# A one-core hybrid encoder layer: the front put in another order (rows turned as they land, indexer first, scoring and heads beside projections, bias table made early)

## The chip, the core and the metric

The kernel runs on one core of one Trainium2 chip. It is written by hand for the core's engines: TensorE multiplies matrices (PE in the profile; PEld is its weight load), VectorE (DVE), ScalarE (ACT) and GpSimd (POOL) do the rest, SyncE (SP) issues most DMAs. The metric is device time in microseconds (us) from start to end of one launch, and the median of several runs is quoted.

## What is computed

One layer of a streaming encoder is applied to 256 prompt rows and 32 sample rows, all in float32 and handled as one block of T = 288 columns. The reference, cut to what matters here:

```python
u = _rmsnorm(x, lw['g_attn'])
zA, zq, zk, zv, ziq, zik, ziw, zmq, zg = _split(u @ lw['w_in'], IN_SIZES)
o_a, new_shift, new_wkv = _rwkv7_time_mix(zA, shift0, wkv0, lw)
...
dots = jnp.einsum('bthd,bsd->bths', iqs, ik_all)
score = jnp.einsum('bths,bth->bts', jax.nn.relu(dots), iws).astype(jnp.float32)
_, idx = lax.top_k(score, topk)
...
logits = jnp.einsum('btngd,btsnd->btngs', qg, ks).astype(jnp.float32) * (HD_B ** -0.5)
bias = rel_bias[_t5_bucket(idx - ps[None, :, None])].astype(jnp.float32)
...
mk, mv = _split(_rmsnorm(mem_prompt, g_mem[l]) @ w_mem_kv[l], (D_M, D_M))
o_m = _memory_attention(zmq.reshape(B, T, H_M, HD_M), mem_k, mem_v)
...
mixed = (gates[:, :, 0] * (o_a @ lw['p_a']) + gates[:, :, 1] * (o_b @ lw['p_b'])
         + gates[:, :, 2] * (o_m @ lw['p_m']))
h = x + mixed @ lw['w_o']
h = h + _hier_moe(_rmsnorm(h, lw['g_ffn']), lw)
```

The change concerns the part up to `o_m`, called the front here: the norm, most of the projection by `w_in`, the projection of the memory rows, the indexer (16 heads score the keys, the best quarter is kept), the 8 attention heads and the 4 heads into the memory.

## The kernel before

**Units of the projections.** A strip is 256 columns of a weight matrix (2 MB). SP loads strips into a ring of four slots, two DMAs of 1 MB each, and loads strip n when the multiplications with strip n - 4 are done. A strip makes two units of 16 matmuls; a unit puts 128 columns of the weights against all 288 rows (for the memory projection 128 memory rows against 256 columns) and is copied out of one of two PSUM banks by ACT. There are 72 units: 16 of the memory projection, 56 of `w_in`. Each matmul is two records in the trace. A quarter of a unit is four matmuls.

**Order before.** (1) The five blocks of rows land whole; ACT squares them, DVE scales them, PE turns them in 80 transposes (line 687), ACT copies them out (lines 1251 and 1253). (2) 16 units of the memory projection (line 703), then 32 transposes of memory keys (line 715). (3) 32 units of `w_in` (line 730). (4) The four memory heads for three blocks of rows (12 turns), with a quarter of one of the last 24 units put between their steps (line 752, `a_mms(1)`, three per turn). (5) The indexer and the heads: for each block of rows 16 scoring matmuls (line 814), whose results ACT clips (1344) and DVE adds up (1589), then top-k in rounds of `max` and `match_replace` on DVE, then 8 heads with two quarters each (lines 821, 829, 845). (6) The norms of the RWKV keys (lines 859 and 867). Then the loop over pairs of RWKV heads begins at line 910, and after it the rest (`p_a`, `w_o` at line 1055, the experts). Between (1) and (6) the engines PE, ACT and DVE wait for each other at the end of each part (`phase_end`, `phase_wait`). The units of the last 24 that carry RWKV columns ("raw" units) are blended by DVE with the row before (`mix`).

**The bias table.** Heads add a bias that depends on the distance of key and query. PE makes 8 rows of 640 numbers from a one-hot table (lines 802 and 803), DVE copies them to `brow`, and POOL writes each row 128 times to DRAM (`dram_bias`) and reads it back with a row pitch one shorter, so that every partition gets its own shift:

```python
pool.wait_ge(s("brow_done"), 1)
pload(dram_bias, brow[0:H_B, :].unsqueeze(1).to_broadcast([H_B, P, BW]), "brow_out")
pool.wait_ge(s("brow_out"), 16)
for h in range(H_B):
    src = bass.AP(tensor=dram_bias.tensor, offset=h * P * BW + 128, ap=[[BW - 1, P], [1, E_W]])
    pload(E[:, h, :], src, "E_in")
```

In part (5) DVE waits for `E_in` (line 1607) before the first head.

## Time and profile before

| | us |
|---|---|
| median of 3 runs (2344.91 to 2354.4) | 2348.91 |
| the profiled execution, its own time | 2346.51 |
| span of the profiled execution | 2344.9 |
| PE busy in it | 2144.5 (91%) |
| DVE, ACT, POOL busy | 536.4, 274.6, 62.9 |
| first record of the RWKV loop (line 910) | 800.37 |

The time outside the span is 1.6 us. A busy engine is one that has an instruction under way; PE's ends are modelled, so 91% is not 91% of its best. The trace also gives the clock that PE was granted: 1.00 is 2.4 GHz and 0.50 is 1.2 GHz.

### The profile page before, as it was taken

The page shows a single profiled execution, that of the slowest core. Times are in us where ns is not written, and L with a number is a line of the kernel's source. Part 1 is how long each engine was busy: PE and PEld are TensorE (multiplying, and loading weights), DVE is VectorE, ACT ScalarE, POOL GpSimd, SP SyncE. Part 2 cuts the span into 40 slices and gives each one's busy share as a digit, 9 for nine tenths or more (in the row PEclk, how much of TensorE's full clock was granted, in tenths as well). Part 3 has the DMA queues.
Part 4 walks back from the last instruction along what each step waited for, and adds up shares of the span by engine and source line. Part 5 has one row for each costly group of instructions (what it writes and reads, how often), then busy time and mean ns, then how long its engine had stood idle before and what let it go on. Part 6 is the DMA issues. An engine that isn't in the chain of part 4 may idle for free.

```text
span 2344.9 us, 30255 instructions
## 1 busy us (share of the span) xinstructions
PE 2144.5 (91%) x12647; PEld 1439.5 (61%) x12647; DVE 536.4 (23%) x1414; ACT 274.6 (12%) x645; POOL 62.9 (3%) x116
## 2 busy tenths in 40 slices
PE   5999999983899899999999999999999699999996
PEld 3887777762675677776767777677777333333332
DVE  1000000222455323232232322322100322122112
ACT  4010000210222201011010101100000100000002
POOL 0000000001000100000000000000000000000000
PEclk9999999995898799999999999999999799999998
DMA  7554434325222113323131322316643399999996
GB/s 237 179 179 144 128 124 123 108 86 104 95 73 65 51 38 113 108 78 113 38 113 60 111 89 76 110 37 241 209 132 137 142 428 427 427 427 427 427 428 273
DMA packets 189048, 404.86 MB, mean 173 GB/s; under 512 B 11328, under 2 KB 165648, under 8 KB 174928
## 3 DMA queue, kind: packets, MB, share of 16 engines
q1 hardware_dynamic: 181136, 380.95, 44.4%
q0 software_dynamic: 6688, 21.20, 3.2%
q8 instruction: 116, 1.90, 0.3%
q10 hardware_dynamic: 1088, 0.66, 0.1%
q14 instruction: 20, 0.16, 0.0%
HBM read 392.10 MB, written 10.67 MB: 172 GB/s over the span
## 4 chain that ended last, share of the span: by engine, by line
PE 81%; DMA 9%; DVE 3%; another core or an unknown queue 2%; issue 2%; ACT 1%; DVEq 1%; ACTq 0%; POOL 0%; SPq 0%
PE bank L891 17%; PE bank L730 11%; PE bank L752 7%; PE bank L1124 6%; PE bank L893 6%; PE bank L1055 5%; PE bank L703 5%; PE bank L1157 3%; PE bank L1174 3%; PE bank L1022 3%; DMA ring<-in_w 3%; DMA Z<-in_w 3%; DMA SC<-in_w 2%; PE bank L947 1%
## 5 line engine op out<-in xcount | busy, mean ns | idle before, releaser
L891 PE MATMUL bank<-uT,ring 128*128 128x288 f32 x1536 | 423.6, 427 | 0.0
L891 PEld LDWEIGHTS bank<-uT,ring 128*128 128x128 f32 x1536 | 292.5, 197 | 86.5 <-issue 5.0
L730 PE MATMUL bank<-uT,ring 128*128 128x288 f32 (+2 forms) x1024 | 248.9, 406 | 0.7 <-ACTq L340 0.7
L730 PEld LDWEIGHTS bank<-uT,ring 128*128 128x128 f32 (+2 forms) x1024 | 190.5, 186 | 58.8 <-ACTq L340 0.9
L752 PE MATMUL bank<-uT,ring 128*128 128x288 f32 x768 | 212.6, 424 | 0.0
L752 PEld LDWEIGHTS bank<-uT,ring 128*128 128x128 f32 x768 | 146.7, 198 | 43.6 <-issue 6.6
L1124 PE MATMUL bank<-ring,Z 128*64 128x512 f32 x480 | 138.5, 611 | 6.9 <-issue 6.9
L893 PE MATMUL bank<-Z,ring 128*128 128x288 f32 x512 | 138.9, 417 | 1.9 <-issue 1.9
L1055 PE MATMUL bank<-SC,ring 128*128 128x288 f32 x512 | 128.4, 409 | 1.1 <-DVEq L340 1.1
L1124 PE MATMUL bank<-Z 128*64 128x512 f32 x336 | 119.2, 614 | 5.0 <-issue 5.0
L1055 PEld LDWEIGHTS bank<-SC,ring 128*128 128x128 f32 x512 | 96.0, 190 | 29.6 <-DVEq L340 1.6
L703 PE MATMUL bank<-ring,Z 128*128 128x256 f32 x512 | 111.0, 379 | 1.9 <-ACT Z L1253 1.3
L893 PEld LDWEIGHTS bank<-Z,ring 128*128 128x128 f32 x512 | 92.7, 190 | 27.0 <-issue 2.8
L1509 DVE TENSOR_TENSOR SC<-SC 128x287 f32<-128x287 f32 (+1 forms) x27 | 12.3, 457 | 423.0 <-ACT SC L1287 373.7
L703 PEld LDWEIGHTS bank<-ring,Z 128*128 128x128 f32 x512 | 97.1, 190 | 15.6 <-issue 1.5
L1386 ACT ACTIVATE Z<-bank 128x288 f32<-128x288 f32 (+1 forms) x48 | 19.7, 410 | 603.1 <-PE bank L891 603.0
L1124 PEld LDWEIGHTS bank<-ring,Z 128*64 128x64 f32 x480 | 43.6, 141 | 72.1 <-issue 72.0
L1124 PE MATMUL bank<-SC,Z 128*64 128x512 f32 x208 | 81.1, 613 | 6.7 <-issue 6.7
L2000 DVE TENSOR_TENSOR uT<-uT,bank 128x512 f32<-128x512 f32 x72 | 49.4, 686 | 142.1 <-PE bank L1174 141.9
L1124 PEld LDWEIGHTS bank<-Z 128*64 128x64 f32 x336 | 35.9, 141 | 51.6 <-issue 51.5
L1022 PE MATMUL bank<-Z,ring 128*128 128x288 f32 x256 | 64.0, 414 | 1.9 <-issue 1.9
L1174 PE MATMUL bank<-SC 128*128 128x512 f32 (+1 forms) x192 | 65.0, 601 | 0.0
(378 smaller groups left out, 2152.0 us busy)
## 6 DMA issues: line engine op xcount, KB each, us to landing
ring<-in_w_in SPq DMA_DIRECT2D x102, 1024.0 KB, 7.7
ring<-in_w SPq DMA_DIRECT2D x42, 2048.0 KB, 31.5
Z<-in_w SPq DMA_DIRECT2D x33, 2048.0 KB, 30.4
SC<-in_w SPq DMA_DIRECT2D x21, 2048.0 KB, 29.4
ring<-in_w_mem_kv SPq DMA_DIRECT2D x16, 1024.0 KB, 9.9
ring<-in_w_o SPq DMA_DIRECT2D x16, 1024.0 KB, 7.6
ring<-in_p_b SPq DMA_DIRECT2D x8, 1024.0 KB, 5.5
ring<-in_p_m SPq DMA_DIRECT2D x8, 1024.0 KB, 8.0
```

The costliest lines, as they stand in the source:

```text
L703: ins = mm(bank[t][:, 0:STRIP], muT[:, c, 128 * t:128 * t + 128], rslot[q][:, c, :], start=c == 0, stop=c == KC - 1)
L730: ins = mm(bank[t][0:w, 0:T], rslot[q][:, c, w0:w0 + w], uT[:, c, :], start=c == 0, stop=c == KC - 1)
L752: ins = mm(bank[t][:, 0:T], rslot[g % 4][:, c, P * t:P * t + P], uT[:, c, :], start=c == 0, stop=c == KC - 1)
L891: ins = mm(b[:, 0:T], rslot[q][:, c, P * t:P * t + P], uT[:, c, :], start=c == 0, stop=c == last - 1)
L893: ins = mm(b[:, 0:T], rslot[q][:, k0 + c, P * t:P * t + P], Z[:, z0 + c, :], start=c == 0, stop=c == last - 1)
L947: ins = mm(bank[2][hs, CH * c:CH * c + CH], Gm[hs, c, 0, 0:CH], TT[hs, 0, c, :], start=True, stop=True)
L1022: ins = mm(bank[n % 2][:, 0:T], wv[:, c, P * t:P * t + P], Z[:, Z_R + c, :], start=c == 0, stop=c == 7)
L1055: ins = mm(bank[m % 2][:, 0:T], rslot[(m // 2) % 4][:, c, P * (m % 2):P * (m % 2) + P], MX[:, c, :], start=c == 0, stop=c == KC - 1)
L1124: ins = mm(bank[2 + w][sides[x], :], XG[:, 8 * h + c, sides[x]], wv[x][:, c, :], start=st < 2 and c == 0, stop=st >= 2 and c == 7)
L1157: ins = mm(bank[4 + b][sides[x], :], HS[:, 2 * h + c, sides[x]], wv[x][:, c, 512 * b:512 * b + 512], start=h == 0 and c == 0, stop=h == 1 ...
L1174: ins = mm(b[p0:p0 + tn, :], GP[:, i % 2, t0:t0 + tn], Yk[:, 512 * g:512 * g + 512], start=True, stop=True)
L2000: ins = V.tensor_tensor(h, h, bank[SCB[n]][:, :], ALU.add)
```

## The change

Everything up to the RWKV loop is written in another order, and the phases between the engines are gone up to the end of `p_a`.

The rows come in four chunks of 512 columns after the constants. PE turns each chunk as it lands, not yet scaled; DVE copies it out with `g_attn`; ACT squares it meanwhile. The scale per row is then spread over the partitions by three matmuls of a diagonal (`dgx`), and DVE multiplies each of the 16 tiles of `uT` by it, signalling tile by tile. The memory rows are loaded after two strips and are turned behind units 1 and 3, and their scale is put into the copy of the projection's result.

The 72 units get a new order: indexer key and weights (units 0 and 1), indexer queries (2 to 9), keys, values and queries (10 to 21), memory projection (22 to 37), memory queries (38 to 45), the RWKV columns (46 to 71). Units 0 to 9 are plain; from there on `filler` hands out quarters. Scoring of all three blocks (sample block first) runs after unit 9 with a quarter after every four scoring matmuls, and four behind each block; the heads of all three blocks run beside units 22 to 45 with four quarters per head; the memory heads beside units 47 to 56; the key norms after them.

The bias table's matmuls stand behind unit 1. POOL starts the write then and reads it back as soon as it is done, into two tables (`ES_b` for the sample block, `EB` of 384 columns for the others). DVE waits for `brow_out` before the scoring, since the table's source and `pen` share space. The cached keys and values are loaded by ACT early, the memory caches by SP after the last head. Behind the RWKV loop one thing changes: the chunks of `x` for the residual are loaded by ACT at the start of the `w_o` stage, where POOL loaded them before that stage.

```diff
+            load(CON[:, :], a["const"][:, 0:NCONST], "con_in")
+            for g in range(4):
+                cs = slice(512 * g, 512 * g + 512)
+                sp.dma_start(X[:, 0:2, cs], a["x_prompt"][0].rearrange("(t p) d -> p t d", p=P)[:, :, cs]).then_inc(xr_in[g], 16)
+                sp.dma_start(X[0:TS, 2, cs], a["x_sample"][0][:, cs]).then_inc(xr_in[g], 16)
...
+            for n in range(2):
+                strip(n, front(n))
+            load(XM, a["mem_prompt"][0].rearrange("(t p) d -> p t d", p=P), "mem_in")
+            for n in range(2, 23):
+                strip(n, front(n))
...
-            phase_wait(pool, 3)
             pload(onehot[0:32, :], a["onehot"], "past_in")
             pload(relb[0:32, :], a["rel_bias"], "past_in")
-            pool.wait_ge(s("brow_done"), 1)
+            pload(vis, a["visible"], "past_in")
+            pool.wait_ge(s("kvt_done"), 1)
...
+            def unit(u, k):
+
+                q, t = (u // 2) % RING, u % 2
+                if k == 0:
+                    if t == 0:
+                        pe.wait_ge(full[q], full_count(u // 2 // RING))
+                    if u >= 2:
+                        pe.wait_ge(*evacuated(u - 2))
+                w0, w = (P * t, P) if u >= 2 else ((0, 80), (80, 32))[u]
+                for c in range(4 * k, 4 * k + 4):
+                    if u == 0:
+                        pe.wait_ge(s("u_done"), c + 1)
...
+            for u in range(U_PLAIN):
+                for k in range(4):
+                    unit(u, k)
+                if u == 1:
+                    pe.wait_ge(s("past_in"), 48)
+                    mm(bank[7][0:H_B, 0:512], relb[0:32, :], onehot[0:32, 0:512], start=True, stop=True)
+                    mm(bank[6][0:H_B, 0:BW - 512], relb[0:32, :], onehot[0:32, 512:BW], start=True, stop=True).then_inc(s("prep_mm"), 1)
+                    pe.wait_ge(s("mem_in"), 16)
+                    mem_turn(0)
+                if u == 3:
+                    mem_turn(8)
...
+            for tt in HEAD_ORDER:
...
+                for h in range(H_I):
+                    hs = slice(64 * (h % 2), 64 * (h % 2) + 64)
+                    if n >= 4:
+                        pe.wait_ge(s("sc_relu"), n - 3)
+                    mm(bank[2 + n % 4][0:tn, 0:L], Z[hs, Z_IQ + h // 2, t0:t0 + tn], ikT[hs, g, 0:L], start=True, stop=True)\
+                        .then_inc(s("sc_mm"), 1)
+                    n += 1
+                    if h % 4 == 3:
+                        fill(1)
+                fill(4)
+            fill(22)
...
+            mix_unit(1)
+            dve.wait_ge(s("prep_mm"), 1)
+            V.tensor_copy(brow[0:H_B, 0:512], bank[7][0:H_B, :])
+            V.tensor_copy(brow[0:H_B, 512:BW], bank[6][0:H_B, 0:BW - 512])
+            dr()
+            dve.sem_inc(s("kvt_done"), 1)
...
+            dve.wait_ge(s("past_in"), 48)
+            dve.wait_ge(s("brow_out"), 16)
...
+            def x_chunk(g):
+
+                cs = slice(512 * g, 512 * g + 512)
+                act.dma_start(XRC[g % 2][:, 0:2, :], a["x_prompt"][0].rearrange("(t p) d -> p t d", p=P)[:, :, cs]).then_inc(xr_in[g], 16)
+                act.dma_start(XRC[g % 2][0:TS, 2, :], a["x_sample"][0][:, cs]).then_inc(xr_in[g], 16)
```

What stands in a row on the engines is shown at three places; a row is the line, the operation, what it writes and reads, and what it waits for. First PE at the start of the program, before the change (the first transposes, and the step to the memory projection):

```order
L687 MATMUL bank<-CON,Z 128x128 [waits x_scaled,con_in]
L687 MATMUL bank<-CON,Z 128x128
L687 MATMUL bank<-CON,Z 128x32
L687 MATMUL bank<-CON,Z 128x128 [waits tr_evac,x_scaled]
L697 UNCONDITIONAL_BRANCH [waits tr_evac]
```

and with it:

```order
L716 MATMUL bank<-CON,Z 128x128 [waits xr_in0,con_in]
L721 MATMUL bank<-SC,CON 128x128 [waits tr_evac]
L739 MATMUL bank<-uT,ring 80x288 [waits u_done,ring_full0]
L739 MATMUL bank<-uT,ring 80x288 [waits u_done] x15
L739 MATMUL bank<-uT,ring 32x288 x16
L765 MATMUL bank<-NK,VEC 8x512 [waits past_in]
L756 MATMUL bank<-CON,SC 128x128 [waits mem_in]
L739 MATMUL bank<-uT,ring 128x288 [waits z_evac,ring_full1]
L739 MATMUL bank<-uT,ring 128x288 [waits z_evac,ring_full2]
L739 MATMUL bank<-uT,ring 128x288 [waits z_evac,ring_full3]
L739 MATMUL bank<-uT,ring 128x288 [waits z_evac,ring_full0]
```

The first transposes wait for the first chunk and no longer for scaled rows; the bias matmuls (line 765) moved ahead of unit 2; the last row shown is unit 8, the first that needs a slot of the ring for the second time.

Second POOL, whose DMAs make the bias table, before the change:

```order
L563 DMA NK<-in_visible 128x512
L563 DMA SC<-in_onehot 32x640 [waits phase_done]
L563 DMA SC<-in_rel_bias 32x8
L563 DMA bias_rows<-SC 1024x1x640 [waits brow_done]
L563 DMA SC<-bias_rows 128x512 [waits brow_out]
L563 DMA SC<-bias_rows 128x512 x7
L582 DMA out_dsa_k_p<-SC 128x2x256 [waits kvt_done]
```

and with it:

```order
L602 DMA NK<-in_onehot 32x640
L602 DMA VEC<-in_rel_bias 32x8
L602 DMA NK<-in_visible 128x512
L602 DMA bias_rows<-NK 1024x1x640 [waits kvt_done]
L602 DMA Z<-bias_rows 32x288 [waits tr_evac,root,brow_out]
L602 DMA Z<-bias_rows 32x288 x7
L602 DMA Z<-bias_rows 128x384 x7
L602 DMA NK<-bias_rows 128x384
L625 DMA out_dsa_k_p<-SC 128x2x256 [waits kvt_done]
```

The write `bias_rows` no longer waits for a phase; its reading back is 16 DMAs where it was 8.

Third PE at the scoring and the first head, before the change:

```order
L814 MATMUL bank<-SC,Z 128x256 [waits prep_done]
L814 MATMUL bank<-SC,Z 128x256 [waits sc_relu] x14
L752 MATMUL bank<-uT,ring 128x288 [waits z_evac]
L752 MATMUL bank<-uT,ring 128x288 x15
L821 MATMUL bank<-Z 128x256
L829 MATMUL bank<-CON,SC 128x128 [waits at_prob]
```

and the scoring with it:

```order
L800 MATMUL bank<-SC,Z 32x288 [waits kvt_done,prep_done,z_evac]
L800 MATMUL bank<-SC,Z 32x288 x3
L739 MATMUL bank<-uT,ring 128x288 x4
L800 MATMUL bank<-SC,Z 32x288 [waits sc_relu] x4
L739 MATMUL bank<-uT,ring 128x288 [waits z_evac]
L739 MATMUL bank<-uT,ring 128x288 x3
L739 MATMUL bank<-uT,ring 128x288 x12
L739 MATMUL bank<-uT,ring 128x288 [waits z_evac,ring_full2]
```

The 16 scoring matmuls of a block stood in one piece and now have a quarter of a unit behind every four; the heads no longer follow their block.

## Rows read from the trace of the kernel before

**Rows 1.** Page, block 1: PE and PEld busy us (share), instructions.

```profile
PE 2144.5 (91%) x12647; PEld 1439.5 (61%) x12647; DVE 536.4 (23%) x1414; ACT 274.6 (12%) x645; POOL 62.9 (3%) x116
```

**Rows 2.** Stretches: us, busy per engine (instructions), granted clock, DMA share, GB/s.

```profile
2.00:42.00 40.00, 16.46 (x61) 10.19 (x62) 6.83 (x9) 23.00 (x35) 0.95 (x3) 1.00 1.04 347
...
412.80:512.80 100.00, 97.72 (x456) 73.75 (x456) 23.13 (x88) 18.89 (x59) 0.00 (x0) 1.00 0.34 106
512.80:592.56 79.76, 27.22 (x95) 16.12 (x95) 22.98 (x65) 8.04 (x25) 10.06 (x17) 0.61 0.52 103
592.56:779.00 186.44, 174.66 (x726) 122.90 (x726) 96.10 (x296) 43.64 (x148) 0.00 (x0) 0.91 0.22 68
779.00:800.37 21.37, 14.79 (x74) 10.27 (x74) 6.46 (x23) 8.22 (x15) 4.01 (x13) 0.60 0.35 109
800.37:815.81 15.44, 15.44 (x43) 9.92 (x43) 6.06 (x16) 3.97 (x9) 2.60 (x5) 0.67 0.05 12
```

**Rows 3.** PE's waits: for whom, us in total, times, longest us.

```profile
PE bank L829 <- DVE SC L1621: 52.3, 4, 44.3
```

**Rows 4.** Chain of the first 165 us: start us, us, what.

```profile
1.93 10.42 DMA Z<-in_x_sample
...
15.84 1.91 ACT SC L1241
...
46.66 55.53 PE bank L703 x256
```

**Rows 5.** Chain of the first 900 us: the 32 units of line 730.

```profile
163.94 248.88 PE bank L730 x1024
```

**Rows 6.** PE in order of time: memory-key transposes, then heads of two blocks.

```profile
158.84 2.18 PE L715 MATMUL bank<-CON,SC 128*128 128x128 f32 x16 [0.57 <-ACT SC L1262]
...
599.10 0.38 PE L829 MATMUL bank<-CON,SC 128*128 128x128 f32 x2
...
604.08 0.38 PE L829 MATMUL bank<-CON,SC 128*128 128x128 f32 x2
...
738.34 0.34 PE L829 MATMUL bank<-CON,SC 32*128 32x32 f32 x3
...
744.19 0.33 PE L829 MATMUL bank<-CON,SC 32*128 32x32 f32 x3
```

**Rows 7.** DVE in order of time: one score added, one round of top-k.

```profile
647.20 0.48 DVE L1589 SCALAR_TENSOR_TENSOR SC<-SC,VEC 128x256 f32<-128x256 f32 x1 [0.20 <-ACT SC L1344]
647.78 0.43 DVE L1596 MAX8 VEC<-SC 128x8 f32<-128x256 f32 x1
...
648.91 0.43 DVE L1596 MAX8 VEC<-SC 128x8 f32<-128x256 f32 x1
```

**Rows 8.** POOL in order of time: the write of the bias table, and reading it back.

```profile
525.17 1.09 POOL L563 DMA_DIRECT2D bias_rows<-SC  x1 [9.19 <-DVEq L1571]
580.01 4.26 POOL L563 DMA_DIRECT2D SC<-bias_rows  x8 [53.74 <-DMA bias_rows<-SC]
```

**Rows 9.** The ring's tile, 545 to 600 us: one strip's two DMAs, and landing.

```profile
L445 SPq DMA_DIRECT2D ring<-in_w_in x2: 372/2488/4604, 548.1 to 548.7; - x2
...
DMA to landing us min/median/max: 9.8/23.2/36.6
```

**Rows 10.** DMA queues, 560 to 572 us: packets, MB, share (POOL's q0, SP's q1).

```profile
q0 software_dynamic: 118, 0.60, 48.2%
q1 hardware_dynamic: 88, 0.09, 2.1%
```

**Rows 11.** Stretches of 2 us around a fall and a rise of the clock.

```profile
518.00:520.00 2.00, 0.30 (x3) 0.22 (x4) 0.55 (x3) 0.00 (x0) 0.00 (x0) 1.00 0.29 58
...
522.00:524.00 2.00, 1.94 (x4) 0.26 (x2) 0.03 (x1) 0.03 (x1) 0.00 (x0) 0.50 0.00 0
...
540.00:542.00 2.00, 2.00 (x7) 1.50 (x7) 1.71 (x6) 0.00 (x0) 0.00 (x0) 0.74 0.46 49
```

**Rows 12.** DMA issues, 1605 to 1622 us: a chunk of x beside weights (us to landing).

```profile
NK<-in_x_prompt POOLq DMA_DIRECT2D x1, 512.0 KB, 7.8
```

More of the change, by code:

```diff
@@ L733, in _ @@
[L733 to L754 removed]
+            pe.wait_ge(s("mk_evac"), 16)
@@ L1246, in _ @@
-            act.wait_ge(s("vec_in"), 16 * N_VEC)
-            for n in range(32):
-                c = n % 16
-                act.wait_ge(s("tr_mm"), n + 1)
-                if n < 16:
-                    ins = A(uT[:, c, :], bank[4 + c % 4][:, 0:T], ACT.Copy, scale=vec["g_attn"][:, c:c + 1])
-                else:
-                    ins = A(muT[:, c, :], bank[4 + c % 4][:, 0:N_MEM], ACT.Copy, scale=vec["g_mem"][:, c:c + 1])
-                ins.then_inc(s("tr_evac"), 1)
-            act.drain()
@@ L1318, in _ @@
-            for i in mem_ends(n)[0]:
-                a_evac(i)
-            phase_end(act, 3)
-            phase_wait(act, 3)
+            A(vec["nmax"][:, 0:1], vec["ss"][:, 0:1], ACT.Sqrt)
+            for g in range(4):
+                act.wait_ge(xr_in[g], 32)
+                for n, (t0, tn) in enumerate(TOK):
+                    act.drain()
+                    A(junk[0:tn, 0:512], X[0:tn, n, 512 * g:512 * g + 512], ACT.Square, accum_out=ssx[0:tn, n, g:g + 1]).then_inc(s("sq_done"), 1)
@@ new lines, in _, with evacs, mem_evac @@
+            fill_step = filler()
+            def evacs(n):
+                for u in finished(fill_step(n)):
+                    evac(u)
+            def mem_evac(c0):
+                for c in range(c0, c0 + 8):
+                    act.wait_ge(s("tr_mm"), KC + c // 2 * 2 + 3)
+                    A(muT[:, c, :], bank[2 + (c // 2) % 4][:, STRIP * (c % 2):STRIP * (c % 2) + STRIP], ACT.Copy,
+                      scale=vec["g_mem"][:, c:c + 1]).then_inc(s("mu_evac"), 1)
+            for u in range(U_PLAIN):
+                evac(u)
+                if u == 1:
+                    mem_evac(0)
+                if u == 3:
+                    mem_evac(8)
+                    for t in range(2):
+                        act.drain()
+                        A(junk, XM[:, t, :], ACT.Square, accum_out=vec["ss"][:, 3 + t:4 + t]).then_inc(s("sq_done"), 1)
+                    act.wait_ge(s("mean_sq"), 2)
+                    A(vec["rs"][:, 3:5], vec["ss"][:, 3:5], ACT.Sqrt).then_inc(s("root"), 1)
@@ new lines, in _, with head_exp @@
+            heads = [(tt, h) for tt in HEAD_ORDER for h in range(H_B)]
+            def head_exp(m):
+                tn = TOK[heads[m][0]][1]
+                L = TP if heads[m][0] < 2 else LS
+                act.wait_ge(s("at_max"), m + 1)
+                A(prob[0:tn, 0:L], lg[0:tn, 0:L], ACT.Exp, bias=vec["nmax"][0:tn, 0:1],
+                  accum_out=vec["sum"][0:tn, 0:1]).then_inc(s("at_exp"), 1)
+            head_exp(0)
+            evacs(2)
+            for m, (tt, h) in enumerate(heads):
+                t0, tn = TOK[tt]
+                act.wait_ge(s("at_tr"), m + 1)
+                if tt == 2:
+                    A(probT[0:TS, 2, 0:tn], bank[5][0:TS, 256:256 + tn], ACT.Copy)
+                A(probT[:, 0:2, 0:tn], bank[5][:, 0:256].rearrange("p (a b) -> p a b", a=2)[:, :, 0:tn], ACT.Copy).then_inc(s("at_pT"), 1)
+                if m + 1 < len(heads):
+                    head_exp(m + 1)
+                evacs(2)
+                act.wait_ge(s("at_pv"), m + 1)
+                A(Z[:, Z_Q + h, t0:t0 + tn], bank[6][:, 0:tn], ACT.Copy).then_inc(s("at_out"), 1)
+                evacs(2 if m + 1 < len(heads) else 0)
@@ new lines, in _ @@
+            act.wait_ge(s("out_kv"), 96)
+            for n in range(16):
+                if n and n % 4 == 0:
+                    evacs(4 if n == 8 else 1)
+                act.wait_ge(s("tr_mm"), 2 * KC + n + 2)
+                A(mkT[:, n // 8, n % 8, :], bank[2 + n % 4][:, 0:N_MEM], ACT.Copy).then_inc(s("mk_evac"), 1)
+            n = 0
+            for tt, (t0, tn) in enumerate(TOK):
+                for h in range(H_M):
+                    act.wait_ge(s("ma_max"), n + 1)
+                    A(prob[0:tn, 0:N_MEM], bank[2][0:tn, 0:N_MEM], ACT.Exp, bias=vec["nmax"][0:tn, 0:1], scale=HD_M ** -0.5,
+                      accum_out=vec["sum"][0:tn, 0:1]).then_inc(s("ma_exp"), 1)
+                    evacs(1)
+                    act.wait_ge(s("ma_tr"), n + 1)
+                    A(probT[:, 0:2, 0:tn], bank[3][:, 0:256].rearrange("p (a b) -> p a b", a=2)[:, :, 0:tn], ACT.Copy).then_inc(s("ma_pT"), 1)
+                    evacs(1)
+                    act.wait_ge(s("ma_pv"), n + 1)
+                    A(Z[:, Z_MQ + 2 * h:Z_MQ + 2 * h + 2, t0:t0 + tn],
+                      bank[4][:, 0:256].rearrange("p (a b) -> p a b", a=2)[:, :, 0:tn], ACT.Copy).then_inc(s("ma_out"), 1)
+                    evacs(1)
+                    n += 1
```

772 lines of the change are left out of this document (369 added, 403 removed).

## The prediction

> **What bounds the kernel now.** I read the page first: PE is busy for 91% of the span [rows 1], so a change of order can only win what PE waits, or what it does at half clock. The stretches come next [rows 2]: the RWKV loop and what follows are touched at one place only, so I look ahead of the loop, in 0 to 800.4 us. There the reader should see three places. The first matmul of a projection starts at 46.66 us [rows 4], because the rows land whole at 12.35, are squared, scaled and turned in series. Then 512.8 to 592.6 us: PE is busy for 27.2 of 79.8 us at a mean clock of 0.61 [rows 2]; one wait of 44.3 us in it, for the first head's probabilities [rows 3], goes back to the bias table, whose write to DRAM takes from 525.2 to 580.0 us [rows 8]. Last 779 to 815.8 us, the key norms and the start of the loop, again with a clock of 0.60 to 0.67 [rows 2]. The order of PE's own work hardly matters beside these: PE is what ends last nearly everywhere else.
>
> **What PE must still do.** The change keeps all 72 units. 56 have 288 columns: 248.88 us for 1024 records [rows 5] is 7.78 us for a unit of 32, and 56 make 435.7 us. 16 have 256 columns: 55.53 us for 8 units [rows 4], 6.94 each, 111.0 us. Together 546.7 us. The rest of PE's work between the first unit and the loop, at full clock:
> - memory rows turned: 32 transposes at 2.18 us for 16 [rows 6], 4.4; bias matmuls (640 columns at 0.43 us for 256, from the 6.94) 1.1, with the small transposes ahead of the scoring 3.3.
> - scoring: 32 matmuls of 256 and 16 of 288 columns by the same rule (0.434 and 0.486 us), 21.7. Before, they were fed at half clock. Quarters between them leave DVE time: an addition starts every 0.6 us at best (0.48 us and a drain [rows 7]), 2.4 us for four, against 1.8 + 1.94 us of PE. Top-k of the first block is 9 rounds of 1.13 us [rows 7], some 10.2, against four quarters and four matmuls and one more quarter, 11.5, before PE needs DVE again. I allow 2.3 us of stalls, 24 in all; from 21.7 up to 34 if the blocks stood in series as far as top-k goes.
> - key and value transposes 2.2.
> - heads: 4.98 us from one head to the next with two quarters (3.89) in it [rows 6], so 1.09 for each of 16; 5.85 in the sample block [rows 6], 1.96 for each of 8; 33.1.
> - memory-key transposes 4.4, and 1.5 for ACT, which copies a little slower than PE turns: 5.9.
> - memory heads: the 100 us of 412.8 to 512.8 [rows 2] hold 36 quarters (70.0), which leaves 30.0.
> - key norms: 14.79 us busy at a clock of 0.60 [rows 2] are 8.9 at full clock; their waits go behind quarters. Last copy 0.6.
>
> That is 4.4 + 3.3 + 24 + 2.2 + 33.1 + 5.9 + 30.0 + 8.9 + 0.6 = 112.4 us.
>
> **When the first unit starts.** The DMA engines move 347 GB/s in the first 40 us [rows 2]. Ahead of the last chunk lie constants 0.69 MB, rows 2.36 MB and some 0.45 MB from POOL: 3.5 MB, 10 us after the start at 2, so 12.5 us (before, the rows were there at 12.35 [rows 4]). ACT's squares cost 1.91 us for 2048 columns [rows 4], so about 0.7 with the accumulator for 512; three are left when the last chunk lands, 14.6. Sum, mean, root, reciprocal, diagonal, three matmuls and the first tile's multiplication are about ten short operations and five hand-overs, 3.9 us: unit 0 starts at 18.5, between 16.5 and 23. Its matmuls take 0.49 us each and the tiles about 0.45, so it is not held up by DVE. PE has pauses here, and in pauses its clock fell: in 518 to 520 us PE worked for 0.3 us at 1.00, and at 522 it was at 0.50; with dense matmuls it was back in 540 to 542 [rows 11]. I add 1.5 us (0 to 6).
>
> **The bias table, moved.** This is the step I trust least. Before, its write ran while PE stood still, and its length set that wait. Now it starts while SP is filling the ring. Unit 1 ends at 18.5 + 1.5 + 15.6 = 35.6. Copy, blend and two copies of `brow` are about 3.1 us (nine operations of 0.1 to 0.7), and the write takes 1.09 + 53.7 us [rows 8]: it ends at 93.5. The scoring, which waits for it, cannot start before unit 9 is done, after 103, so that wait is covered; without the cover it would cost what is left of the 54.8 us. But look at the strip that SP asked for at 548 us, in the middle of the write: its first MB landed after 9.8 us, its second after 36.6 [rows 9], that is at 585, some 5 us behind the end of the write. In 560 to 572 us SP's queue moved 88 packets and 0.09 MB beside POOL's 118 packets and 0.60 MB [rows 10]: the write holds its engines with large packets, and the strip gets one small packet for one large one. The share of 0.48 is about half of the 16 engines, filled by a write from 8 partitions. Everything up to strip 3, the memory rows and the caches included, is 13.5 MB: at 347 GB/s from 2 us on that is done at about 41, just as the write begins. Strip 4 is asked for at 35.6 and so lies behind them: I let it land 5 us behind the write, at 98.5. Unit 8 needs it at 35.6 + 1.1 + 4.4 + 6 x 7.78 = 87.8. PE waits 10.5 us and loses about 1 us to the clock: 11.5, from 0 (the strip is through by then) to 24 (rivals). Strips 5 and 6 follow at 6 us each and are not late.
>
> The Trainium skill ("DMA: Bandwidth & Descriptors", Queues, rings and completion order) says that each engine goes round the queues by packets and drains a whole packet of some 9 to 17 descriptors before it switches. By that a strip would be through long before unit 8, and the sum would be 11.5 us less; of [rows 10] the trace bears out the round, not the size of the turn.
>
> **What else moves.** The units' copies stay on ACT, which had 18.9 us of work in the 100 us from 412.8 on [rows 2] and works in order; each unit has two banks and 7.8 us, so I cost these at nothing; without that cover a copy is 0.4 us. Memory keys for the sample block are loaded after the last head: 1 MB, some 6 us, behind 11.9 us of transposes and five quarters; uncovered, 6. At the loop's start PE needed 15.44 us up to the first Gram matmul [rows 2], half of it at half clock; at full clock DVE's chain of about 10.7 is the longer: -4.7. Behind the loop, chunk 0 of x is now asked for at the start of `w_o` beside two 2 MB loads; PE needs it one unit and no more, 7.8 us, later. Beside such loads a chunk took 7.8 us [rows 12]: +1.5 (0 to 4).
>
> **Sum.** The loop starts at 18.5 + 1.5 + 546.7 + 112.4 + 11.5 = 690.6 instead of 800.4: -109.8. With -4.7 and +1.5 it is -113.0. Against the profiled execution's own 2346.5 that is 2233.5; that execution lies 2.4 below the median of the three runs, whose spread is 10, so I say 2234.
>
> **Rivals.**
> - The broadcast does not starve the ring. For it: the first MB of that strip did land in 9.8 us [rows 9]. Against it: the second. Then 11.5 us less, 2222. (The Trainium skill's rule named above gives this time.)
> - It starves strip 3 too, if the first 13.5 MB take longer than 41 us. Unit 6 needs strip 3 at 87.8 - 15.6 = 72.2, and it comes at about 95: 22.8 us and 1 of clock instead of 11.5, while strip 4 then is in time: +12, 2246. For it: only a margin of a few us, and 4096 short runs in strip 0. Against it: about 1 MB got through after the write had begun [rows 9].
> - On the other side: PE stays at 1.2 GHz from its first unit on, because its early work comes in short pieces. A unit then costs 7.78 us more; the gain of 113 is gone after 14.5 units, and from 16 units on the kernel is slower by over 0.5%. For it: in 784 to 810 us, fed in pieces, PE stayed low (0.60 and 0.67 in [rows 2]). Against it: dense matmuls brought the clock back soon after 540 [rows 11], and units 0 to 7 are dense.
> - The order is right but DVE or ACT, now in one long program without phases, holds a hand-over at many turns: 1 us at each of the 24 heads and 12 memory turns is 36 us, 2270. Against it: in those stretches PE was busy for 97.7 of 100 us [rows 2] with half the quarters between the same steps.
>
> **How the numbers follow.** 0.5% (12 us) is about what a measurement here can tell. Chances: forecast 0.48 (own range 2224 to 2244), no starving 0.18, two strips starved 0.17, hand-overs 0.12, half clock 0.02, anything else 0.03. The range 2212 to 2262 takes in the first three with the bounds of the start (-2 to +4.5), scoring and the chunk, and part of the fourth. Only the half clock ends above the old time, and part of the rest: faster 0.96, same 0.02, slower 0.02.
>
> **What would show it.** Right: first record of the units at 17 to 23 us; a wait of PE for the ring of 5 to 15 us near 88, and none longer ahead of the loop; the write's end near 93; scoring at a clock of 1.00; the loop's first record near 691; memory heads and key norms without idle. Wrong: a wait for the ring near 72; a wait at the first score for `brow_out`; a clock of 0.5 beyond 30 us; PE idle at `w_o` for more than 4 us.

## The result and the profile after

The changed kernel takes 2196.46 us (median of 4 runs, 2194.33 to 2196.79) against 2346.91 for the kernel before: a ratio of 0.9353, 95% interval 0.9337 to 0.9369. It is faster, and 15.5 us below the lower end of the range that was forecast. Its profiled execution took 2194.33 us with a span of 2192.5.

The page first, of the kernel after; its first line answers [rows 1]:

```profile
PE 2083.6 (95%) x12653; PEld 1408.8 (64%) x12653; DVE 544.8 (25%) x1446; ACT 274.2 (13%) x648; POOL 63.3 (3%) x116
...
PEclk9999999999999999999999999999998999999999
...
q8 instruction: 55, 0.90, 0.2%
```

The last line (packets, MB, share of the DMA engines) has a counterpart that the forecast does not use. It is this line of the page of the kernel before:

```profile
q8 instruction: 116, 1.90, 0.3%
```

The kernel after fetches half as many packets of instructions, though PE runs about as many instructions. That leads to the larger part of what the forecast missed.

Where the time came from, by spans: the loop's first record was at 800.37 and is at 678.37 (-122.0; forecast -109.8). The loop lasts 780.7 us instead of 811.5 (-30.8; forecast -4.7). The rest is 0.4 longer (forecast +1.5). Together 2344.9 - 152.4 = 2192.5.

Stretches of the kernel after, in the columns of [rows 2]: the start, units 0 to 9, the scoring, the memory heads, the key norms, the loop's start:

```profile
0.00:27.16 27.16, 15.59 (x55) 8.89 (x55) 10.05 (x27) 10.36 (x27) 2.55 (x9) 1.00 1.02 281
27.16:117.50 90.34, 90.34 (x385) 65.43 (x385) 9.05 (x34) 15.60 (x35) 9.27 (x17) 1.00 0.77 190
117.50:170.90 53.40, 53.06 (x249) 35.37 (x248) 39.21 (x100) 18.29 (x50) 0.00 (x0) 1.00 0.47 149
...
447.00:543.00 96.00, 95.60 (x449) 72.39 (x449) 24.47 (x94) 18.13 (x57) 0.00 (x0) 1.00 0.30 94
545.00:580.30 35.30, 34.38 (x169) 25.58 (x168) 6.81 (x22) 9.52 (x16) 2.74 (x6) 0.95 0.28 88
...
678.37:693.86 15.49, 14.99 (x153) 11.72 (x155) 7.21 (x21) 4.39 (x10) 3.16 (x6) 1.00 0.48 150
```

The wait of 44 us at the first head [rows 3] and the half clock around it are gone: from 27 us on PE is busy in every stretch. Units 0 to 9 have no idle time at all, so the wait for the ring that the forecast put near 88 us did not come. PE's three longest waits ahead of the loop are these (for whom, us in total, times, longest):

```profile
PE bank L716 <- DMA Z<-in_x_sample: 8.8, 1, 8.8
PE bank L721 <- DVEq L1581: 2.1, 1, 2.1
PE bank L903 <- ACT Z L1430: 0.9, 1, 0.9
```

The start is later than forecast. PE in order of time: the rows turned, the mean squares spread over the partitions, units 0 and 1:

```profile
8.82 13.80 PE L716 MATMUL bank<-CON,Z 128*128 128x128 f32 x48 [8.82 <-DMA Z<-in_x_sample]
24.74 1.78 PE L721 MATMUL bank<-SC,CON 128*128 128x128 f32 x6 [2.12 <-DVEq L1581]
27.16 18.02 PE L739 MATMUL bank<-uT,ring 128*80 128x288 f32 x64 [0.64 <-DVE uT L1585]
```

Turning takes 13.8 us, 0.86 for each of 16 chunks, and units 0 and 1 take 18.0 instead of 15.6. The trace has no clock record of this execution before 31.6 us (a stretch without one shows 1.00), but 0.86 is the duration at 1.2 GHz, as the experiment with idle products ahead of the rows shows below (8 chunks in 7 us at a clock of 0.50).

Two more things are late here: the last of the rows, and the squares on ACT. Landing of the last part of the last chunk, asked for at 5.15 us, and ACT's last record on the squares:

```profile
Z<-in_x_sample SPq DMA_DIRECT2D x1, 64.0 KB, 9.8
```

```profile
18.33 0.18 ACT L1294 ACTIVATION_READ_ACCUMULATOR SC<-Z 32x1 f32 x1
```

The rows are there at 14.9 (forecast 12.5) and the squares at 18.5 (forecast 14.6), so without the half clock the turning would no longer end last, but the squares still would, 3.9 us behind the forecast.

The bias table was forecast well. POOL writes it from 48.16 us, and it is done at 102.80:

```profile
48.16 1.08 POOL L602 DMA_DIRECT2D bias_rows<-NK  x1 [44.20 <-DVEq L1630]
102.80 7.65 POOL L602 DMA_DIRECT2D Z<-bias_rows  x15 [53.56 <-DMA bias_rows<-NK]
```

That is 54.6 us, 15 us ahead of the first score at 117.5. It also kept a strip back, as in [rows 9], but another one. Below are the two DMAs of strip 4 and of strip 5, each with the landing times of both:

```profile
L441 SPq DMA_DIRECT2D ring<-in_w_in x2: 367/475/583, 45.2 to 45.6; - x2
...
DMA to landing us min/median/max: 5.4/6.9/8.5
```

```profile
L441 SPq DMA_DIRECT2D ring<-in_w_in x2: 368/2600/4832, 63.8 to 64.2; - x2
...
DMA to landing us min/median/max: 9.9/26.5/43.0
```

Strip 4 was asked for 3 us ahead of the write and landed by 54.1. Strip 5 was asked for inside it, and its second MB landed at 107.2, 4.4 us after the write's end. Unit 10 needed it at 113.5, so nobody waited.

Then the loop, which the change does not edit. It makes eight turns, one for each pair of heads. Stretches of one turn each, four of the kernel before and then two of the kernel after:

```profile
902.30:1004.45 102.15, 97.43 (x845) 72.53 (x845) 29.74 (x74) 10.70 (x21) 3.77 (x7) 0.97 0.27 86
1004.45:1104.74 100.29, 95.75 (x846) 71.60 (x846) 29.73 (x74) 10.70 (x21) 3.77 (x7) 0.98 0.28 88
1104.74:1203.47 98.73, 94.14 (x846) 70.58 (x845) 29.75 (x74) 10.70 (x21) 3.77 (x7) 1.00 0.28 89
1305.69:1407.36 101.67, 97.43 (x845) 72.45 (x844) 29.75 (x74) 10.70 (x21) 3.77 (x7) 0.97 0.27 86
```

```profile
775.71:873.05 97.34, 94.19 (x846) 70.50 (x845) 29.74 (x74) 10.71 (x21) 4.00 (x7) 1.00 0.28 89
873.05:970.40 97.35, 94.18 (x845) 70.49 (x844) 29.75 (x74) 10.71 (x21) 4.01 (x7) 1.00 0.28 89
```

The work is the same, yet turns took 98.7 to 102.2 us and now take 97.34. The beginning of the second turn shows why. PE in order of time, before:

```profile
902.30 0.51 PE L910 MATMUL bank<-Z 64*128 64x288 f32 x1
...
905.10 0.64 PE L912 MATMUL bank<-Z 128*128 128x288 f32 x2 [2.04 <-issue]
...
907.33 8.92 PE L891 MATMUL bank<-uT,ring 128*128 128x288 f32 x24
```

and after:

```profile
775.71 0.51 PE L962 MATMUL bank<-Z 64*128 64x288 f32 x1
...
776.39 0.75 PE L964 MATMUL bank<-Z 128*128 128x288 f32 x2
...
778.24 8.03 PE L943 MATMUL bank<-uT,ring 128*128 128x288 f32 x32
```

Before, PE's array stopped for 2.04 us behind the first two matmuls of the turn, released by nothing but "issue" (no other engine and no transfer that the profile shows), and then worked at 1.2 GHz from 906.3 to 913.1 us (24 matmul records in 8.92 us, now 32 in 8.03). A wait of this kind stands in every turn but the first; PE's waits there in the kernel before (us in total, times, longest):

```profile
PE bank L912 <- issue: 13.1, 7, 2.2
```

In the second turn the queue of instruction packets shows nine packets; in the kernel after it shows none from 766 us, late in the first turn, to the end of the loop.

### The profile page after: what moved, and what is told of

Read it like the earlier page. It is cut to its first block, busy times and chain, and to the rows that moved or that the text cites. A ratio compares the mean times of both kernels' runs of the same rounds, so it can differ in the third digit from the quotient of the medians.

```text
span 2192.5 us, 30178 instructions
## 1 busy us (share of the span) xinstructions
PE 2083.6 (95%) x12653; PEld 1408.8 (64%) x12653; DVE 544.8 (25%) x1446; ACT 274.2 (13%) x648; POOL 63.3 (3%) x116
## 4 chain that ended last, share of the span: by engine, by line
PE 83%; DMA 9%; DVE 3%; issue 2%; DVEq 1%; ACT 1%; ACTq 0%; SPq 0%
PE bank L739 20%; PE bank L943 15%; PE bank L1176 6%; PE bank L945 6%; PE bank L1107 5%; PE bank L737 5%; PE bank L1209 3%; PE bank L1226 3%; PE bank L1074 3%; DMA ring<-in_w 3%; DMA Z<-in_w 3%; DMA SC<-in_w 3%; PE bank L999 1%; PE bank L1007 1%; PE bank L1008 1%
## 5 line engine op out<-in xcount | busy, mean ns | idle before, releaser
L739 PE MATMUL bank<-uT,ring 128*128 128x288 f32 (+2 forms) x1792 | 454.8, 410 | 0.6 <-DVE uT L1585 0.6
L943 PE MATMUL bank<-uT,ring 128*128 128x288 f32 x1536 | 407.2, 414 | 0.0
L739 PEld LDWEIGHTS bank<-uT,ring 128*128 128x128 f32 (+2 forms) x1792 | 333.3, 189 | 99.5 <-issue 8.0
L943 PEld LDWEIGHTS bank<-uT,ring 128*128 128x128 f32 x1536 | 281.9, 190 | 78.7 <-issue 3.1
L737 PE MATMUL bank<-ring,Z 128*128 128x256 f32 x512 | 117.4, 382 | 0.0
L945 PEld LDWEIGHTS bank<-Z,ring 128*128 128x128 f32 x512 | 92.7, 189 | 27.0 <-issue 2.8
L1840 DVE TENSOR_TENSOR SC<-SC,bank 128x320 f32<-128x320 f32 x72 | 32.2, 484 | 106.8 <-PE bank L1008 106.8
L1074 PEld LDWEIGHTS bank<-Z,ring 128*128 128x128 f32 x256 | 48.6, 190 | 15.7 <-issue 2.4
L1209 PE MATMUL bank<-ring,SC 128*64 128x512 f32 x192 | 49.5, 594 | 7.5 <-DMA SC<-in_w 3.9
```

The source lines that it names most:

```text
L737: ins = mm(bank[t][:, 0:STRIP], muT[:, c, P * t:P * t + P], rslot[q][:, c, :], start=c == 0, stop=c == KC - 1)
L739: ins = mm(bank[t][0:w, 0:T], rslot[q][:, c, w0:w0 + w], uT[:, c, :], start=c == 0, stop=c == KC - 1)
L943: ins = mm(b[:, 0:T], rslot[q][:, c, P * t:P * t + P], uT[:, c, :], start=c == 0, stop=c == last - 1)
L945: ins = mm(b[:, 0:T], rslot[q][:, k0 + c, P * t:P * t + P], Z[:, z0 + c, :], start=c == 0, stop=c == last - 1)
L1074: ins = mm(bank[n % 2][:, 0:T], wv[:, c, P * t:P * t + P], Z[:, Z_R + c, :], start=c == 0, stop=c == 7)
L1209: ins = mm(bank[4 + b][sides[x], :], HS[:, 2 * h + c, sides[x]], wv[x][:, c, 512 * b:512 * b + 512], start=h == 0 and c == 0, stop=h == 1 ...
```

## The experiments

All times are medians; the kernel before, run beside each set, took 2348.2 to 2351.0. The changed kernel's ratio, to compare with, is 0.9353.

**The loop's code.** Theory A: what was gained in the loop comes from where its code lies. Theory B: it comes from the new order. One pass of the loop is some 1740 PE instructions. Counting each PE instruction ahead of the loop once (a loop of the front is run twice in the kernel before), the trace has 5558 before and 6082 after, 524 more, which is two blocks of 256 and 12. In the kernel before PE runs some 10 or 11 instructions of the turn before it stops. If it stops at the end of a block, the loop began about 11 ahead of that end and now begins about one behind it. Four kernels shift it. (The Trainium skill, "Runtime: NRT & Kernel Launch", Instruction fetch mechanics, states that an engine's instruction memory, 2048 instructions for PE, is refilled in 16 KiB blocks of 256 instructions, and that a taken branch whose target is not in the current window of two pages forces a fetch. The trace agrees with the size: nine packets are shown as 0.15 MB. It does not agree with the window: in the changed kernel seven packets come in the first turn and none in turns 2 to 8, so some 1740 instructions stayed.)

The kernel before, with 16 instructions more:

```diff
             pe.wait_ge(s("con_in"), 16)
+            for _ in range(8):
+                nc.tensor.transpose(bank[7][0:32, 0:32], ident[0:32, 0:32], ident[0:32, 0:32])
```

> The kernel before, with eight idle 32x32 transposes (16 instructions) ahead of PE's first wait for the rows, where it waits anyway. Theory A (place of the loop's code): the RWKV loop's body is 1740 PE instructions, and in the kernel before it begins some 11 instructions ahead of the end of a 16 KB block of code, spans 8 blocks, does not stay on the chip and is fetched again in each turn; 16 instructions move its start just past the end of the block, it spans 7 and stays. Then no instruction packets inside the loop after its first turn (now 9 in a turn), turns of 97.3 us instead of 98.7 to 102.2, and the time falls by some 26 us, from 2347 to 2321 (2315 to 2326). Theory B (the new order of the front is what makes the loop faster, through the clock or the transfers with which it enters the loop): nothing changes, 2347 within 5.

Measured: 2320.7 us, ratio 0.988 (0.9857 to 0.9904). The first turn takes 101.8 us, all others 97.4, seven instruction packets come in the first turn and none later. The third turn:

```profile
1000.30:1097.70 97.40, 94.21 (x846) 70.53 (x845) 29.78 (x74) 10.71 (x21) 3.77 (x7) 1.00 0.29 89
```

Eight idle transposes give the old kernel 27 us. Theory B falls for turns 2 to 8; what it keeps is the first turn, 4.4 us longer with PE at 1.2 GHz, which the forecast had.

The changed kernel with its loop moved back (it leaves out four products of the last projection unit):

```diff
-                for c in range(4 * k, 4 * k + 4):
+                for c in range(4 * k, 4 * k + (0 if (u, k) == (71, 2) else 4)):
```

> The changed kernel without four of the sixteen products (16 PE instructions, 1.9 us) of the last projection tile, so one tile of the output is incomplete. Theory A: the loop's code moves back by 16 instructions, to some 15 ahead of the end of a block; 9 instruction packets in each turn return, with PE's wait of 1.4 to 2.2 us behind the loop's first two matmuls and, in most turns, a stretch at 1.2 GHz. Turns of 98.7 to 102.2 us instead of 97.34: 2196.5 - 1.9 + 7 x 4.2 = 2224 (2208 to 2232). Theory B: 2194.6, within 3.

Measured: 2207.2 us, ratio 0.9395 (0.937 to 0.9421). Some nine packets a turn are back, and so is the wait, 0.8 to 1.65 us; PE in order of time:

```profile
772.61 0.75 PE L964 MATMUL bank<-Z 128*128 128x288 f32 x2
774.86 0.64 PE L965 MATMUL bank<-Z 32*128 32x288 f32 x2 [1.50 <-issue]
```

The wait stands behind the products of line 964; in the kernel before it stood ahead of the same products (line 912). That is some four instructions later, as the count has it (12 forward and 16 back). Turns take 98.1 to 99.9 us. With the 1.9 us left out some 12 us are lost, just under what was expected, because the clock fell in two of the turns only, for 3.4 us each (before: in six of seven, in four of these for 6.8).

Two shifts forward, at one place of the changed kernel (16 transposes, and 50 in the second):

```diff
+            pe.wait_ge(s("tr_evac"), KC)
+            for _ in range(16):
+                nc.tensor.transpose(bank[7][0:32, 0:32], ident[0:32, 0:32], ident[0:32, 0:32])
             pe.wait_ge(s("tr_evac"), KC + 1)
```

> The changed kernel with 16 idle transposes (32 instructions) in PE's wait for the root mean square. Theory A: the body's 1740 instructions leave 52 of 7 blocks, so from a start one or two instructions into a block a shift by 32 still lets it stay: turns of 97.34, time 2196 to 2198. A narrower form of theory A, in which the loop's first instruction has to stand at a block's edge, would give the turns of before, 2225. Theory B: 2196 to 2198.

Measured: 2197.35 us, ratio 0.9357, no packets after the first turn: the body still fits.

> The changed kernel with 50 idle transposes (100 instructions) at the same place, some 1.6 us of them not hidden. Theory A: the body spans 8 blocks again and is fetched again in each turn (8 or 9 packets). What that costs tells two forms apart. If the cost lies in the fetch behind the branch (PE's sequencer stood 3.8 us there in the kernel before, and runs some 4.3 us ahead of the array), the array waits 0 to 1 us in a turn and keeps its clock: 2198 to 2206. If any fetch at the branch costs what it cost before, 2196.5 + 1.6 + 29 = 2227. Theory B: 2198.

Measured: 2197.28 us, ratio 0.9356. Some nine packets in every turn, and still turns of 97.35 without a wait:

```profile
776.00:873.35 97.35, 94.19 (x846) 70.50 (x845) 29.75 (x74) 10.71 (x21) 4.02 (x7) 1.00 0.29 90
```

So the fetch alone costs nothing here. PE's sequencer, which reads the instructions ahead of the array, stands at the branch that ends a turn. The branch's records in this kernel (83 ns: the last one, which leaves the loop) and in the changed one:

```profile
L926 PEldq COMPARE_BRANCH  x8: 83/3506/3796, 771.7 to 1453.0; - x8
```

```profile
L923 PEldq COMPARE_BRANCH  x8: 76/215/247, 771.4 to 1452.7; - x8
```

In all kernels that fetch it stands 3.3 to 3.9 us, in the others 0.2; but it reached the branch 4.3 us before the array got there. The array waits where the block that holds the branch's target ends a few instructions later, so that the sequencer has to stand again for the next one before it has a new lead. That is read from three kernels: the wait comes some 11 and 15 instructions into the turn where the count above puts the end of the block there, and not at all where it leaves 155. This second stand, and the half clock that often follows, was the price before.

**The start and the ring.** Theory S: the rows are turned at 1.2 GHz. Theory R: the ring was spared only because of the late start.

```diff
+            pe.wait_ge(s("ss_init"), 1)
+            for _ in range(8):
+                mm(bank[7][:, 0:T], uT[:, KC - 1, 0:P], uT[:, KC - 1, :], start=True, stop=True)
             pe.wait_ge(s("con_in"), 16)
```

> The changed kernel with eight idle 128x288 products on a zeroed tile while PE waits for its first rows (1.4 to 8.8 us). Theory S (the late start is PE's clock: the 48 transposes of the rows ran at 1.2 GHz, 0.86 us for a chunk of three): at 2.4 GHz a chunk takes 0.43, the rows' squares on ACT become what ends last (18.5), and unit 0 starts at about 22 us instead of 27.2, unit 1 ends at about 38 instead of 45.1. Rival S' (the start is bound by the landing of the rows or by VectorE's copies): unit 0 stays at 27 us and the time at 2196. Theory R (there was no wait for the ring only because of the late start: strip 4 was asked for at 45.2 us, 3 us ahead of the bias write at 48.2, when the queue had just run empty): with unit 1 ending at 38, strip 4 is asked for behind 3 to 4 MB that are still under way, its second MB lands some 5 us after the end of the write, near 100, and PE waits about 10 us for it at unit 8. S and R together: 2196.5 - 7 + 11 = 2200 (2194 to 2205), with that wait. S without R: 2189, without it.

Measured: 2196.45 us, ratio 0.9347 (0.9331 to 0.9362). The time is the rival's, but unit 0 started at 25.3, where neither forecast had it (22 and 27): PE turned the first four chunks at 0.55 us each and then lost its clock again. Stretches of this kernel while it turns:

```profile
6.50:12.00 5.50, 4.42 (x23) 2.67 (x22) 2.05 (x5) 2.82 (x8) 0.00 (x0) 1.00 1.05 317
14.00:21.00 7.00, 6.75 (x24) 3.52 (x23) 4.26 (x9) 4.09 (x12) 0.00 (x0) 0.50 1.27 238
```

At 0.50 it turned 8 chunks in 7 us, 0.86 each, which is the changed kernel's duration. Unit 1 ended at 43.4 instead of 45.1, too little to test R (strip 4 landed after 8.7 us).

The same with `pool.wait_ge(full[0], 64)` ahead of POOL's write:

> The same idle products, and POOL holds the bias write until strip 4 has landed. S and R: unit 0 at 22 us, no wait at unit 8; the write runs from some 50 to 105, now it is strip 5 that lands 4 to 5 us after its end, near 110, and unit 10 needs it at 106: a wait of up to 5, and the scoring, which waits for the write's end, begins no later than that. 2189 to 2195. Without S: 2197 to 2202.

Measured: 2194.88 us, ratio 0.9331 (0.9315 to 0.9347), no wait for the ring; not told apart from the kernel without the hold. In its profiled execution the write ended at 108.9 and strip 5 at 112.8: again 4 us behind it.

R by itself, with the start left alone:

```diff
             for n in range(2, 23):
+                if n == 4:
+                    sp.wait_ge(s("z_mm"), 3)
                 strip(n, front(n))
```

> The changed kernel in which SP asks for strip 4 one unit later, at some 56 us instead of 45.2, so 8 us behind the start of the bias write instead of 3 ahead of it. Theory R (the write starves SP's queue, and the forecast's wait did not come only because strip 4 was asked for just ahead of it): strip 4's second MB lands 4 to 5 us behind the end of the write, near 107; unit 8 needs it at 96.5, PE waits 10 to 11 us and loses about 1 to the clock, and all behind it moves: 2196.5 + 11.5 = 2208 (2204 to 2212). Rival (the write does not keep a strip back for 50 us; strip 5 was late because of its place in the queue): the strip lands some 10 us after it is asked for, no wait, 2196.5.

Measured: 2209.51 us, ratio 0.9404 (0.9388 to 0.9419). Landing of the strip's two DMAs, asked for at 56.5 and 57.0 us, and PE at unit 8:

```profile
DMA to landing us min/median/max: 9.9/30.2/50.5
```

```profile
107.51 17.60 PE L741 MATMUL bank<-uT,ring 128*128 128x288 f32 x64 [10.45 <-DMA ring<-in_w_in]
```

The forecast's wait of 10.5 us, where it had put it, behind strip 4. Eleven us decide: asked for at 45.2 us, 3 ahead of the write, it lands in 8.5; at 56.5, 8 behind the write's start, in 50.5. (The rule weighed in the prediction, of the Trainium skill's "DMA: Bandwidth & Descriptors", Queues, rings and completion order, would have had such a strip through long before unit 8; this run is against it.)

Now with products between the transposes too:

```diff
+                mm(bank[c % 8][:, 0:P], uT[:, KC - 1, 0:P], uT[:, KC - 1, 0:P], start=True, stop=True)
                 for n, (t0, tn) in enumerate(TOK):
                     ins = nc.tensor.transpose(bank[c % 8][:, t0:t0 + tn], ...
...
+            for _ in range(6):
+                mm(bank[7][:, 0:P], ident, ident, start=True, stop=True)
```

> The kernel with eight idle products ahead of the rows' transposes, which gained 1.7 us: PE rose to 2.4 GHz at 6.1 us and fell again at 12.9, amid the transposes. Now also one idle 128x128 product ahead of each chunk's three transposes and six in the wait for the root. Theory S (transposes alone do not hold the clock, products between them do): a chunk takes 0.43 + 0.22 = 0.65 us instead of 0.86, the turning ends near 19.5 instead of 22.6, units 0 and 1 take 15.6 us instead of 18: unit 1 ends at 38 to 40 instead of 45.1; without a wait for the ring 2190, with theory R's wait for strip 4 (asked for at 39, behind what is still under way) 2196 to 2201. If the clock falls all the same, a chunk takes 1.3 us: 2200 to 2206.

Measured: 2192.47 us, ratio 0.9335 (0.9319 to 0.9351). The clock stays up (14 to 21 us, and unit 0):

```profile
14.00:21.00 7.00, 7.00 (x45) 5.12 (x43) 4.37 (x9) 4.18 (x12) 0.00 (x0) 1.00 1.27 240
...
25.60 15.84 PE L746 MATMUL bank<-uT,ring 128*80 128x288 f32 x64 [0.64 <-DVE uT L1593]
```

Units 0 and 1 take 15.8 us, unit 1 ends at 41.4. A product costs 0.33, so a chunk takes 0.81 and little is won in the turning itself. R's wait, forecast for so early an end of unit 1, did not come. Landing of strip 4's two DMAs, asked for at 41.5 and 41.9 us:

```profile
DMA to landing us min/median/max: 7.3/14.0/20.7
```

The strip is there at 62.6, in the middle of the write (44.4 to 99.9): it took longer than the 8.5 us of the changed kernel, but it was not held to the write's end. Strip 4 is asked for when unit 1 ends, and the write starts some 3 us behind that, in this kernel as in the changed one. So the write can hold a strip back for its whole length, but the late start is not what spared strip 4, down to an end of unit 1 at 41.4. This kernel and the next are the fastest of the study, 4 us under the changed kernel, which the intervals don't tell apart from it.

> The same, and POOL holds the bias write until strip 4 has landed. S and R: strip 4 lands before 52, the write runs to about 106, strip 5's second MB lands near 110 and unit 10 needs it at 107: 2190 to 2195, with a wait of 0 to 4 at unit 10. If the clock falls all the same: 2202 to 2208.

Measured: 2192.39 us, ratio 0.9336 (0.932 to 0.9351), with a wait of 1.5 us for strip 5.

The last of this group makes that product 32 columns wide and writes the bias table from 128 partitions:

```diff
-            pload(dram_bias, brow[0:H_B, :].unsqueeze(1).to_broadcast([H_B, P, BW]), "brow_out")
+            pload(dram_bias.rearrange("h (r i) w -> (h r) i w", i=H_B), brow.unsqueeze(1).to_broadcast([P, H_B, BW]), "brow_out")
```

> The kernel with idle products between the transposes (2192.5), with two edits. The product ahead of each chunk has 32 columns instead of 128, which should take a chunk from 0.81 us to some 0.65 and unit 1's end from 41.4 us to about 39, if PE keeps 2.4 GHz. And the bias rows are made on 128 partitions (the eight heads repeated 16 times by the matmul itself) and written from there, 8 copies each, instead of from 8 partitions with 128 copies. Theory R': the write took 54 us because its 8 source partitions keep half the engines busy and that is also why a strip starves; spread over all of them it takes 27 us or less, and strip 4, asked for at 39, lands before unit 8 needs it at 90, without a wait: 2190 (2187 to 2193). If the write's length does not depend on the partitions, strip 4 is 10 us late: 2200. If the clock falls between the smaller products: 2196 to 2200.

Measured: 2199.6 us, ratio 0.9352 (0.9339 to 0.9365). Two edits, two answers. With 32 columns the clock fell at 12.3 us, chunks took 1.29, and unit 1 ended at 50.2, 8.8 later than in the kernel that this one is built on. But the write:

```profile
53.23 0.89 POOL L603 DMA_DIRECT2D bias_rows<-NK  x1 [49.26 <-DVEq L1642]
66.88 7.72 POOL L603 DMA_DIRECT2D Z<-bias_rows  x15 [12.76 <-DMA bias_rows<-NK]
```

13.7 us instead of 54.6: R' holds for the write's length. For the strips it is not tested. The six strip DMAs issued from 50 to 90 us landed in 6.9 us in the middle, 12.6 at most, but none of them was asked for while the write ran: two at 50.3 and 50.7, ahead of it, and the next at 69.0, behind its end.

**Two parts of the change undone.** First POOL also waits for `s("z_mm")` to reach `U_PLAIN` ahead of the bias write:

> One part of the change undone: the bias write waits until the ten plain units are done (some 112 us) instead of starting at 48. If the order of the bias table is worth its whole uncovered length, VectorE's wait for the end of the write stands in front of the scoring until 112 + 54.6 = 167, and PE, which can score about six heads ahead, waits some 47 us: 2244 (2235 to 2256, the upper half with a stretch at 1.2 GHz behind the wait). If other work fills that time (the rival), under 2215.

Measured: 2248.05 us, ratio 0.9563 (0.9547 to 0.9579), with this wait at the scoring:

```profile
PE bank L801 <- ACT SC L1372: 47.5, 2, 47.2
```

An early table is worth its uncovered length, about a third of what the change brings. Then the quarters between the heads of the scoring go behind each block, on PE and ACT:

```diff
-                    if h % 4 == 3:
-                        fill(1)
-                fill(4)
+                fill(8)
```

> One part undone: the quarters of projection units that stand between the heads of the scoring stand behind each block of 16 heads instead. VectorE adds a head in 0.6 us (0.48 and a drain), PE scores one in 0.34: some 4 us of waits in each of three blocks, 12 in all, and with them perhaps a stretch at 1.2 GHz: 2205 to 2213. If the interleaving is worth nothing because the eight quarters behind cover it: 2196 to 2199.

Measured: 2208.37 us, ratio 0.9393 (0.9378 to 0.9409), 9 to 12 us lost. The scoring's matmuls, in this kernel and then in the changed one:

```profile
L800 PE MATMUL bank<-SC,Z 64*128 64x256 f32 (+1 forms) x96 | 24.7, 434 | 0.2
```

```profile
L800 PE MATMUL bank<-SC,Z 64*128 64x256 f32 (+1 forms) x96 | 15.1, 407 | 0.3 <-ACT SC L1371 0.3
```

The waits hide in the first row's busy time: a block of 16 heads takes 8.1 to 8.2 us, 0.5 each, since the weight loads wait for ACT (33 times, 12.0 us in all) and ACT in part for DVE (13 times, 3.0 us).

## Why the prediction failed

The sign and the order of size were right, the number not. By its own steps:

- **The loop: this step failed.** The prediction says that the RWKV loop is "touched at one place only" and prices that place at -4.7. The place is right (4.6 off the first turn; the old kernel with 16 instructions more keeps a first turn 4.4 longer than the others). But turns 2 to 8 became 26 us shorter, and that is nothing the new order does: eight transposes give the old kernel the same. The wait for "issue" in each turn, the clock of 0.97 and the 116 instruction packets were all in the profile before. Without these 26 us the time would have been some 2222.6, inside the range. From the shifted old kernel, 2320.7, to the changed one it is -124; the forecast for the front, the loop's start and the chunk was -113.
- **When the first unit starts: too early by 9.6.** Forecast 18.5 and 1.5 for the clock; measured 27.2 and 2.4. The rows' turning was thought to hide behind the landing, and the clock's loss to be 1.5; at 0.86 us a chunk it ends at 22.6, 7.7 us behind the last landing (14.9). Only some 4 us of the lateness is the clock's, by estimate: the rows landed 2.4 late and ACT needs 0.8 for a square where 0.7 was charged, so the squares alone, done 3.9 late, would have moved the start by as much.
- **The ring: mechanism right, strip wrong, -11.5.** The write's length (54.6, forecast 54.8) and a strip's landing 4 to 5 us behind it came true, and a strip 4 asked for inside the write costs the wait that was forecast (10.45; the forecast's 98.5 less 87.8 is 10.7, not 10.5). What failed is that strip 4, asked for 3 us ahead of the write, would be held: it landed at 54.1. Strip 5 was held, with 6 us to spare. How much of that the late start did is open: with unit 1's end at 41.4 strip 4 got through too, and no run has the 35.6 of the forecast. That this error and the late start nearly cancel in the sum is luck.
- **What PE must still do: 10.3 too much.** The units need 546.7 as forecast, to about 1 us; the rest took 102 and not 112.4. Most of it is the scoring, 16.5 instead of 24 (53.3 us from the first score to the last, less 4.75 units of 7.76): the products of two neighbouring heads lie on rows 0 to 63 and 64 to 127 and run at the same time (their records start within 0.01 us of each other), 15.1 us for 48 of them (0.31) where 0.43 and 0.49 were charged. Reckoned like the scoring, by what their quarters leave, memory heads come to 28.0 (30.0), memory keys 4.3 (5.9), key norms 12.1 (8.9).
- **The chunk of x:** a wait of 1.0, forecast 1.5.
- **Rivals.** Hand-overs on DVE or ACT: no wait over 1 us between the first unit and the loop. PE at half clock from its first unit: only to 31.6 us. Two strips starved: strip 3 was in time. No starving of a needed strip: so it went, but not because the write starves none (strip 5 was held).

What stays open: why the clock fell after waits of 1.6 to 2.2 us in six turns of the old kernel and not after 1.4 in the seventh, while in the changed kernel less 16 instructions it fell after two waits of 1.4 and not after one of 1.65. That the bias write's length depends on how its 1024 rows are spread over source partitions is shown; whether the short write still holds a strip back that is asked for inside it, and why about 1 MB gets through the long one first, is not.

## What to carry to other kernels

A stage that an edit does not touch can still change, because its code moves: where a long loop shows waits for "issue" behind its branch and instruction packets in every turn, shift its start by some idle instructions before crediting or blaming anything else. A transfer that starves a queue is priced by who asks just after it, so an error of some ten microseconds in an early time can decide whether the wait exists at all: forecast such a term with both outcomes. And try a broadcast to DRAM from many partitions: here that made it four times as fast.

## What the hardware showed that was not expected

- A loop of some 1740 PE instructions stayed on the chip (7 packets in its first turn, then none) or was fetched again in every turn (some 9 packets), depending on where it began. The price of fetching was 0 with some 155 instructions left in the target's block (counted as above), some 12 us over seven turns with about 15, and 26 with about 11.
- PE rose to 2.4 GHz at 6.1 us, after idle products, and fell to 1.2 at 12.9 while it turned rows. It stayed up in the run with a 128x128 product ahead of every three transposes, and fell in the one with 128x32.
- The same 2.6 MB took 54.6 us from 8 partitions with 128 copies of each row and 13.7 us from 128 partitions with 8.
